# Two unused gaps, of 40 and 24 bytes, in the on-chip address map of a two-block transformer kernel

## The reference, cut to what matters

```
h = x + concat(dilated attention, gated recurrence)(rmsnorm(x)) @ w_out
h = h + cross_attention(rmsnorm(h), rmsnorm(mem))
h = h + square(relu(rmsnorm(h) @ w_mlp_in)) @ w_mlp_out
x = rmsnorm(h) * norm_final_g
```

```
z = rmsnorm(x) @ w_in                       # 1024 x 6944
merged = sum over n of sigmoid(gate_n) * (mixer_n(z) @ w_branch[n])
x = x + merged @ w_out
x = x + (silu(h2 @ w_gate) * (h2 @ w_up)) @ w_down,   h2 = rmsnorm(x)
```

## The kernel before, in words

| buffer | start, bytes | start modulo 64 | bytes |
|---|---|---|---|
| ring | 16512 | 0 | 24576 |
| w_hi, w_lo | 41088, 57472 | 0, 0 | 16384 each |
| const | 73856 | 0 | 11528 |
| vec | 85408 | 32 | 544 |
| row | 85952 | 0 | 8192 |
| h (the residual), xs | 94144, 102336 | 0, 0 | 8192 each |
| x_hi, x_lo | 110528, 118720 | 0, 0 | 8192 each |
| oT | 126912 | 0 | 8192 |
| W (the work area) | 135104 | 0 | 88080 |
| junk, stat | 223200, 225248 | 32, 32 | 2048 each |
| rrow | 227296 | 32 | 1024 |

## Time and profile before

### The profile page before, as it was taken

The page is one execution under the profiler, slowest core; times in us unless marked ns, Lnnn a source line. Parts: engine busy times, 40 slices in busy tenths (PEclk is TensorE's granted clock), DMA queues, the critical chain, the costliest instruction groups (busy, mean ns, idle before and its releaser), DMA issues.

```text
span 1293.7 us, 22072 instructions
## 1 busy us (share of the span) xinstructions
PE 1265.9 (98%) x9208; PEld 1178.1 (91%) x9208; DVE 862.2 (67%) x1194; ACT 652.5 (50%) x1049; POOL 114.4 (9%) x152
## 2 busy tenths in 40 slices
PE   8999999999999999998999999999999999999998
PEld 8998999988788989997999998888899988999986
DVE  6897667644466675998656553667577996655543
ACT  5896655543368464342544443556552434544432
POOL 1100000000000000661000000000003810000000
PEclk8999999999999999999999999999999999999999
DMA  9543445555535323442555555433343325455552
GB/s 368 204 163 115 180 135 192 196 185 180 188 101 193 131 99 131 164 152 84 189 189 176 190 196 185 165 139 136 112 145 131 134 96 196 165 191 174 187 196 98
DMA packets 30324, 211.77 MB, mean 164 GB/s; under 512 B 3344, under 2 KB 3728, under 8 KB 5264
## 3 DMA queue, kind: packets, MB, share of 16 engines
q1 hardware_dynamic: 29936, 210.22, 45.5%
q10 hardware_dynamic: 288, 0.14, 0.0%
HBM read 209.29 MB, written 1.05 MB: 163 GB/s over the span
## 4 chain that ended last, share of the span: by engine, by line
PE 74%; DVE 13%; ACT 6%; issue 5%; DMA 1%; SPq 0%; DVEq 0%; ACTq 0%
PE bank L508 72%; DVE w_lo L1625 3%; ACT w_hi L1125 2%; DVE W L1599 2%; DMA ring<-weight_pieces 1%; ACT W L1125 1%; PE bank L608 1%; PE bank L843 1%; DVE xs L2125 1%; DVE W L1585 1%; DVE junk L2123 1%; DVE W L2105 1%; DVE W L1586 1%; DVE W L1617 0%; DVE stat L1558 0%
## 5 line engine op out<-in xcount | busy, mean ns | idle before, releaser
L1625 DVE TENSOR_TENSOR w_lo<-ring,w_hi 128x2048 fp32r<-128x2048 f32 x183 | 422.5, 2309 | 283.9 <-ACT w_hi L1125 283.5
L1125 ACT ACTIVATE w_hi<-ring 128x1024 fp32r<-128x1024 f32 (+1 forms) x368 | 366.2, 1046 | 241.9 <-PE bank L508 226.2
L508 PE MATMUL bank<-x_hi,w_hi 128*128 128x256 f32 x1840 | 267.2, 284 | 2.4 <-ACT w_hi L1125 2.4
L508 PE MATMUL bank<-x_hi,w_lo 128*128 128x256 f32 x1840 | 261.5, 281 | 1.0 <-DVE w_lo L1625 0.9
L508 PE MATMUL bank<-x_lo,w_hi 128*128 128x256 f32 x1840 | 254.8, 280 | 0.0
L508 PEld LDWEIGHTS bank<-x_hi,w_hi 128*128 128x128 f32 x1840 | 237.0, 189 | 5.7 <-issue 2.4
L508 PEld LDWEIGHTS bank<-x_hi,w_lo 128*128 128x128 f32 x1840 | 236.5, 188 | 2.3 <-DVE w_lo L1625 1.7
L508 PEld LDWEIGHTS bank<-x_lo,w_hi 128*128 128x128 f32 x1840 | 233.6, 188 | 0.0
L508 PE MATMUL bank<-W 128*128 128x128 f32 (+4 forms) x716 | 110.7, 327 | 8.3 <-ACT W L1125 4.8
L508 PEld LDWEIGHTS bank<-W 128*128 128x128 f32 (+3 forms) x716 | 87.8, 187 | 21.5 <-issue 12.3
L508 PE MATMUL bank<-w_lo,hid_hi 128*128 128x512 f32 x304 | 78.5, 394 | 0.0
(11 more groups left out here) (257 smaller groups left out, 1238.0 us busy)
## 6 DMA issues: line engine op xcount, KB each, us to landing
ring<-weight_pieces SPq DMA_DIRECT2D x191, 1024.0 KB, 4.8
const<-constants SPq DMA_DIRECT2D x1, 1376.5 KB, 8.9
W<-x_features SPq DMA_DIRECT2D x4, 256.0 KB, 5.2
ring<-weight_pieces SPq DMA_DIRECT2D x2, 512.0 KB, 6.0
h<-x SPq DMA_DIRECT2D x2, 512.0 KB, 11.9
W<-rg_weights SPq DMA_DIRECT2D x1, 1024.0 KB, 9.7
xs<-mem_features SPq DMA_DIRECT2D x1, 1024.0 KB, 11.4
oT<-mem SPq DMA_DIRECT2D x1, 1024.0 KB, 11.4
```

What stands on the lines that cost most here:

```text
L508: return nc.tensor.matmul(out, lhsT, rhs, start=first, stop=last)
L1125: return nc.scalar.activation(out, in_, ACT.Copy, scale=scale)
L1625: v.tensor_tensor(w_lo[:, q % SPLITS, 0:n], raw(pp)[:, 0:n], w_hi[:, q % SPLITS, 0:n].bitcast(F32), ALU.subtract).then_inc(s_weight_low, 1)
```

## The change

Two buffers that nothing reads or writes are allocated, one of 10 fp32 (40 bytes) in each partition before `ring`, one of 6 fp32 (24 bytes) before `h`. Nothing else is changed: the instructions, their order, the waits and the transfers are the same, with other addresses. The change is described as moving every buffer to an address that is a multiple of 64 bytes.

```
             return ctx.enter_context(nc.semaphore(name))
 
+        sb("to_64_bytes", [P, 10])
         ring = sb("ring", [P, RING, PIECE])
         w_hi = sb("w_hi", [P, SPLITS, PIECE], F32R)
         w_lo = sb("w_lo", [P, SPLITS, PIECE], F32R)
         const = sb("const", [P, C_SIZE])
         vec = sb("vec", [P, V_SIZE])
         row = sb("row", [P, R_SIZE])
+        sb("to_64_bytes_again", [P, 6])
         h = sb("h", [P, TT, D])
         xs = sb("xs", [P, TT, D])
         x_hi = sb("x_hi", [P, KT, S], F32R)
```

## The result

The changed kernel takes 1307.1 us in the median of four runs (1306.22 to 1309.19), the kernel before 1295.42 us (1294.65 to 1296.40). The ratio is 1.0092, with a 95% interval of 1.0075 to 1.0110: slower by 0.9%, 12 us, outside the range of the forecast. The profiled execution took 1309.19 us with a span of 1307.4 us, 13.7 us more than the span before.

A forecast was written before the change was run, and what follows sets the result against it. It took matmul and weight-load durations to bound the kernel, with a VectorE and ScalarE chain in the mixers. All terms were 0: 1295.53 + 0 = 1295.5 us, 1295.2 us for a median; range 1293.0 to 1298.5.

The forecast's parts named there:

- The addresses: Allocator sums: `ring` and weights move 64 bytes, everything from `h` on 96, putting activations 32 past a multiple of 64.
- the TensorE one: 7632 fast fp32 matmuls with a moved operand: bounded by 1 ns each way, 5.6 us on the chain, taken as 0.
- Rival B: Slower, 15%: activations at 32 past a multiple of 64 cost TensorE 1 ns in each of 7632 matmuls; 1300.8 us.
- Its own sign: Matmul groups with `x` or `hid` 1 ns or more longer, or wide layers 2 us or more, mixers unchanged.
- Rival C: Faster, 9%: simultaneous accesses of TensorE, or TensorE and VectorE, meet less often on one half of 64 bytes; 1289.6 us.
- The share on the chain: Of the 7.6 us bound on extra TensorE work, 74% was counted as on the chain: 5.6 us.
- The spread: Runs of this kernel were said to differ by 0.08%, a measurement telling 0.2%, 2.6 us, from no change.
- The other terms: VectorE at most 0.8 us, ScalarE 0.5 us either way, contention 0.2 us, transfers -19% to 0 of 2.6 us; each taken 0.
- The rule on how transfers are cut at multiples of 256 bytes: Transfers on the chain: +0.1 us for `ring` pieces, -0.1 us for the store of `h`, together 0.

The follow-up runs named there:

- e16: The kernel before with only the first gap of the change (40 bytes before `ring`); 1294.86 us, ratio 1.0010.
- e17: The kernel before with only the second gap of the change (24 bytes before `h`); 1306.78 us, ratio 1.0108.
- e3: The kernel before with `ring`, weights and everything else down to `W` starting at 32 past a multiple of 64; 1292.65 us, ratio 0.9995.
- e4: The kernel before with only `w_hi` and `w_lo` moved to 32 past a multiple of 64, activations at 0; 1306.59 us, ratio 1.0104.
- e1: The kernel before with gaps that make every buffer really start at a multiple of 64 bytes; 1300.86 us, ratio 1.0056.
- e2: The kernel before with only `x_hi` and `x_lo` moved to 32 past a multiple of 64; 1306.11 us, ratio 1.0095.
- e8: The kernel before with `x_hi` and `x_lo` 16 bytes further from the weights, `W` with `hid` 64 further; 1304.97 us, ratio 1.0077.
- e5: The kernel before with everything from `h` on 128 bytes further from the weights; 1287.74 us, ratio 0.9947.
- e14: The kernel before with `x_hi` and `x_lo` 128 bytes further from the weights, `W` with `hid` 192 further; 1285.10 us, ratio 0.9940.

## Why the prediction was wrong

**The addresses were right.** The sums on the allocator held: e16 and e17 do what the starts worked out for them say, and the change moved the activations by 32 bytes more than the weights.

**The step that failed is the TensorE one**: "The difference is 1 ns or, once, in favour of the odd start. I bound it by 1 ns each way", and "The value I take is 0". The measured price was 2.2 ns for each of the 5520 matmuls that move `x_hi` or `x_lo` (2.1 by their busy time), 1 ns for each of the 912 with `hid`, and about 2.3 ns for 1152 of the 1200 with stationary `x_hi` or `x_lo` (busy time up 0.3, 1.4 and 0.9 us in their three groups). Two things were wrong in it. The neighbours were plain fp32 matmuls, and the rows after show that these don't react: the 256 that move `oT` past `ring` follow each other at 215.8 ns before and after, and at 215.8 to 216.0 ns in every other profile here, at all the distances. I had written that no fast fp32 row existed at 32 and still took the bound from another kind of instruction. And the question put to the rows was the wrong one: I sorted them by where an operand starts, while what counts is how two operands stand to each other, which no single-operand row can show.

**Rival B had the direction and the engine, with the wrong mechanism and half the size.** It gave 1300.8 us against 1307.1. It was priced by the start of an operand; e3 and e4 refute that, e1 too. Its price of 1 ns was the same false bound. Its own sign, that the mixers keep their length, didn't hold either: on the chain the first wide layer starts 1.9 us later than before, and the stretches from one wide layer to the next are 2.8 and 0.8 us longer, for 2640 of the 5520 matmuls lie outside the wide layers (at 2.2 ns each 5.8 us). Rival C had named the two simultaneous accesses of TensorE, but with the wrong sign.

**The share on the chain was too low.** I let 74% of the extra work count; of 15.1 us busy time 13.7 us reached the span, 91%. The wide layers hang on TensorE wholly, and in the mixers more of the chain now runs through TensorE: VectorE and ScalarE went from 19% to 17% of it.

**The spread was too narrow.** I took 0.08% from three runs. Later runs of the same kernel lie between 1288.85 and 1296.94 us, 0.6%. The measured loss is clear of that.

**The other terms were right.** VectorE's and ScalarE's lines kept their durations, `w_lo` its 2293 ns, the pieces land after 4.8 us and the store of `h` after 2.6 us as in the earlier trace rows. The rule on how transfers are cut at multiples of 256 bytes (the Trainium skill, "DMA: Bandwidth & Descriptors", "How a descriptor splits into AXI transactions") came to 0.1 us of a landing time that is read to 0.1 us; no run here shows it.

**What stays open.** That the two things that meet are TensorE's load of the next weights and its reading of the moving operand is an inference: the rhythm depends on the distance between exactly these two buffers, it survives without the writers, and e2 and e4 have different distances from the loaded `ring` to `x_hi` (+32 and +64) with the same rhythm. It was not measured with TensorE alone. Open too are why each distance has the rhythm it has, what lets an execution fall into 113.3 ns for a layer and why that happens more often at +128, why `hid` at +64 has 232.4 ns in e1 and 233.3 in e8, and 224 bytes, the one multiple of 32 not tried.

## What to carry to other kernels

When TensorE works without idle time in fast fp32 matmuls, the distance between its stationary and its moving operand is worth trying as a tuning knob: from the worst to the best place in this kernel it was 1.7% of the whole (0.9940 to 1.0108), for gaps that cost nothing else. Distances of up to 256 bytes were tried, and +256 was as 0; no other kernel was. Read it in the profile by the time from one run of matmuls to the next, not by their mean duration, and try the multiples of 32 for each pair of operands. Conversely, an edit that changes the size of a buffer between such a pair can shift the time (here by between 0.6% down and 1.1% up), so two kernels are compared fairly only at the same distances. And when no row shows the kind of instruction on which a change acts, the rows of another kind don't bound it.

## What the runs showed of the hardware that was not expected

- Fast fp32 matmuls of 256 columns that move `x` past the weights followed each other at 113.3, 117.8, 117.3 to 118.7 or 120.0 ns (layer means) at the full clock, by the distance of their operands; those of 512 columns at 226.7 to 234.3 ns. A distance of +256 bytes gave the same as 0. Plain fp32 matmuls (382 and 378 ns, 57.7 and 7.2 us in all) were the same before and after.
- The two roles differ: with `x` moving past the weights, +192 bytes gave 120 ns, with the weights moving past `hid` the same +192 bytes gave the best spacing, 226.7 ns.
- At one distance two rhythms are possible: at 0, 117.8 ns in the profile of before and 113.3 ns in one layer of e3. At +128 both profiled executions (e5 and e14) had 113.3 ns in the first wide layer and 117.8 ns in most of the later two.
- A fast fp32 matmul took no harm from an operand that starts 32 bytes past a multiple of 64 (e3, 0.9995), nor did a VectorE or ScalarE operation.
